# Constant matmuls ahead of the first transposes, and a new order of the first stage's roots, copies and modulation columns

## The reference

```python
c_act = jax.nn.silu(c)                                   # (1, 1024)
mod = c_act @ ada_w[layer] + ada_b[layer]                # (1, 6144)
sh1, sc1, g1, sh2, sc2, g2 = split(mod, 6)
h = rms_norm(x) * (1.0 + sc1) + sh1                      # x: (1024, 1024)
proj = h @ w_in                                          # queries, keys, values, output gate, 8 gate columns
```

## Time and profile before

| | us |
|---|---|
| three runs | 1089.71, 1090.55, 1092.70 (median 1090.55) |
| the profiled execution, its own time | 1091.59 |
| its span | 1089.7 |
| PE busy | 1074.5 (99%) |
| DVE busy | 727.2 (67%) |
| ACT busy | 447.5 (41%) |
| POOL busy | 168.1 (15%) |

### The profile page before, as it was taken

The page is one execution under the profiler, slowest core; times in us unless marked ns, Lnnn a source line. Parts: engine busy times, 40 slices in busy tenths (PEclk is TensorE's granted clock), DMA queues, the critical chain, the costliest instruction groups (busy, mean ns, idle before and its releaser), DMA issues.

```text
span 1089.7 us, 14684 instructions
## 1 busy us (share of the span) xinstructions
PE 1074.5 (99%) x5146; PEld 902.6 (83%) x5146; DVE 727.2 (67%) x1282; ACT 447.5 (41%) x824; POOL 168.1 (15%) x149
## 2 busy tenths in 40 slices
PE   6999999999999999999999999999999999999997
PEld 6888888888888888888888888888888888888886
DVE  6846767577479637888667665766666465844666
ACT  7852232222224316764343343334333325544445
POOL 3752322212326523310000000000000000000000
PEclk9999999999999999999999999999999999999999
DMA  9425352432432523115545435453553879665553
GB/s 377 170 77 162 116 197 80 140 114 61 160 116 64 189 78 129 66 39 203 158 142 198 169 107 192 146 168 131 191 177 106 299 270 395 223 194 193 192 155 155
DMA packets 86969, 177.10 MB, mean 163 GB/s; under 512 B 8152, under 2 KB 31320, under 8 KB 85872
## 3 DMA queue, kind: packets, MB, share of 16 engines
q1 hardware_dynamic: 85984, 174.80, 47.2%
q0 software_dynamic: 480, 1.09, 0.4%
q10 hardware_dynamic: 432, 0.27, 0.1%
HBM read 135.97 MB, written 40.16 MB: 162 GB/s over the span
## 4 chain that ended last, share of the span: by engine, by line
PE 97%; DVE 1%; ACT 1%; DMA 0%; issue 0%; DVEq 0%
PE OP L2360 27%; PE OP L2061 21%; PE O L2360 15%; PE ST L2360 5%; PE DC L2360 5%; PE AD L2360 5%; PE O L2061 3%; PE ST L2061 3%; PE AD L2061 2%; PE DC L2061 2%; PE O L2216 1%; PE O L2232 1%; PE DC L2232 1%; PE ST L2199 1%; PE OP L2135 1%; PE ST L2085 0%
## 5 line engine op out<-in xcount | busy, mean ns | idle before, releaser
L1826 DVE TENSOR_TENSOR dL<-dF,dH 128x1024 fp32r<-128x1024 f32 x77 | 93.0, 1223 | 69.1 <-ACT dH L1216 68.2
L2061 PE MATMUL OP<-wH,hH 128*128 128x512 f32 (+1 forms) x360 | 135.0, 375 | 0.1
L2061 PE MATMUL OP<-wH,hL 128*128 128x512 f32 (+1 forms) x360 | 132.1, 367 | 0.0
L2061 PE MATMUL OP<-wL,hH 128*128 128x512 f32 (+1 forms) x360 | 131.7, 366 | 0.0
L1216 ACT CAST dH<-dF 128x1024 fp32r<-128x1024 f32 x77 | 80.0, 1052 | 89.2 <-DMA dF<-w_units 42.6
L2360 PE MATMUL OP<-tH,wsH 128*128 128x512 f32 x264 | 102.7, 389 | 0.0
L2360 PE MATMUL OP<-tL,wsH 128*128 128x512 f32 x264 | 102.7, 389 | 0.0
L2360 PE MATMUL OP<-tH,wsL 128*128 128x512 f32 x264 | 102.7, 389 | 0.0
L2061 PEld LDWEIGHTS OP<-wH,hL 128*128 128x128 f32 x360 | 67.8, 188 | 11.3
L2061 PEld LDWEIGHTS OP<-wH,hH 128*128 128x128 f32 x360 | 67.9, 188 | 10.3 <-issue 0.3
L2061 PEld LDWEIGHTS OP<-wL,hH 128*128 128x128 f32 x360 | 67.9, 189 | 10.0
(11 more groups left out here) (341 smaller groups left out, 2645.5 us busy)
## 6 DMA issues: line engine op xcount, KB each, us to landing
raw<-w_units SPq DMA_DIRECT2D x76, 512.0 KB, 4.7
dF<-act_mid SPq DMA_DIRECT2D x77, 256.0 KB, 2.8
ada<-ada_rest SPq DMA_DIRECT2D x64, 256.0 KB, 2.9
wst<-w_units SPq DMA_DIRECT2D x44, 256.0 KB, 4.9
down_mid<-wst SPq DMA_DIRECT2D x22, 512.0 KB, 3.2
dF<-down_mid SPq DMA_DIRECT2D x44, 256.0 KB, 3.0
dF<-w_units SPq DMA_DIRECT2D x33, 256.0 KB, 6.1
ada<-ada_first SPq DMA_DIRECT2D x8, 1024.0 KB, 10.1
```

What stands on the lines that cost most here:

```text
L1826: nc.vector.tensor_tensor(dL[g][:], dF[g][:], dH[g][:].bitcast(F32), ALU.subtract).then_inc(d_L, 1)
L2061: ins = nc.tensor.matmul(out_ap, lhs[a], rhs[b], start=(n == 0 and i == 0), stop=(last and i == 2))
```

## The change

Five edits, all in the first stage:

- PE multiplies a tile of ones by itself 14 times (128 x 128 float32, into bank `OP0`, which the gates' products overwrite later), as soon as the constants stand and before it waits for row tile 0 (`WARM`).
- ACT does `root(t)` directly behind `square(t)`, ahead of the copy of row tile `t - 2`.
- The copy of row tile 7 out of the first bank goes from ACT to DVE, which then does both copies of that tile. DVE waits for ACT's copy of row tile 6 before it, since both count on one semaphore.
- The last product step and the closing addition of `sum1(1)` go behind DVE's three copies of row tiles 6 and 7.
- PE does `mod_columns(1)` behind the products of `k` = 0 and half 0, not ahead of them.

```diff
+WARM = 14
@@ ACT
                 square(t, xin[:, t, :])
+                root(t)
                 if t >= 2:
                     evac_xT(t - 2)
-                root(t)
             act.wait_ge(b1_ok, 1)
             mod_columns(0)
             modulate(0, 0)
             evac_xT(NT - 2)
-            evac_xT(NT - 1)
             modulate(0, 1)
@@ DVE
-            def evac_xT(t):
+            def evac_xT(t, j=1):
 
-                dve.wait_ge(n_tr, 2 * t + 2)
-                nc.vector.tensor_copy(four_of(xnT, 1, t),
-                                      XT_BANKS[2 * (t % 2) + 1][:].rearrange("p (k n) -> p k n",
-                                                                             n=P)).then_inc(xT_ok[1], 1)
+                dve.wait_ge(n_tr, 2 * t + j + 1)
+                nc.vector.tensor_copy(four_of(xnT, j, t),
+                                      XT_BANKS[2 * (t % 2) + j][:].rearrange("p (k n) -> p k n",
+                                                                             n=P)).then_inc(xT_ok[j], 1)
@@ DVE
-            sum1(1, 6)
+            sum1(1, 6, 7)
             evac_xT(NT - 2)
+            dve.wait_ge(xT_ok[0], NT - 1)
+            evac_xT(NT - 1, 0)
             evac_xT(NT - 1)
+            sum1(1, 7)
@@ PE
+                for _ in range(WARM):
+                    nc.tensor.matmul(OP[0][:, 0:P], ones[:], ones[:], start=True, stop=True)
                 for t in range(NT):
                     pe.wait_ge(n_hn, t + 1)
@@ PE
-                mod_columns(1)
                 pe.wait_ge(wg_L, 1)
@@ PE
                         if last:
                             ins.then_inc(gates_mm, 1)
+                        if k == 0 and half == 0:
+                            mod_columns(1)
```

## The result

| | before | changed |
|---|---|---|
| runs, us | 1089.71 to 1092.70, median 1091.09 (6) | 1092.86 to 1095.72, median 1094.99 (6) |
| profiled execution, own time | 1091.59 | 1092.86 |
| its span | 1089.70 | 1090.99 |

The ratio is 1.0034, 95% interval 1.0024 to 1.0044: slower by 3.7 us (2.6 to 4.8). I had forecast 1090.6 and a range of 1088.9 to 1092.2. The profiled execution of the changed kernel is the fastest of its six, 1.27 us over that of before. So its trace can show only a part of the loss; the mean granted clocks of the six are 0.999 for this one and 0.996 to 0.998 for the others.

What follows compares the result with a forecast made beforehand. TensorE was taken to bound the kernel (97% of the span). Terms -1.23, +1.16 and +0.12 gave +0.05 us on a median of 1090.55, so 1090.6, range 1088.9 to 1092.2.

Steps and rivals of the forecast that it cites:

- the paragraph on half 0: First products of k = 0: GpSimd's first weights land at 20.44 as before, products start at 25.65 against 26.88, 1.23 us earlier.
- the sum I had made: First stage: -1.23 (half 0 earlier), +1.16 (new wait ahead of k = 1), +0.12 (GpSimd's hL of k = 2), giving +0.05 us.
- The chain behind it: From first product at 25.65: moved columns at 27.60, ScalarE reads at 28.24, GpSimd starts at 30.24, k = 1 at 31.59.
- The fallen clock: TensorE idle between rows, products and k = 1: the clock falls between 24 and 32, costing 2.6 us, 1093.2; chance 0.09.
- the 5.3 us of the start: Slow-clock stretch after TensorE's first pass, to about 14.0; half speed that long was taken to cost 2.6 us.
- Constants done before row 0, rows 0 and 1 fast: TensorE's start: 28 constant passes end by 8.2, the clock rises at about 7.5, rows 0 and 1 save 2.5 us.
- Row 7's end at 23.8 to 24.3: TensorE's last row transposes end then, against 26.06 before.
- VectorE's copy of row 7 done by 24.6 to 24.9: Moved copy: bank full at 23.1 to 23.6, copies of rows 6 and 7 take 0.6 to 0.7 each.
- the constants don't do what they say: Rival: clock still rises at about 14, rows end as now, k = 1 at 32.0; 0.4 slower, 1091.0; chance 0.05.
- GpSimd as the bound for k = 2 and 3: Rival: GpSimd limits these products, everything some tenths later, +0.4 to +1.0, 1091.0 to 1091.5; chance 0.07.
- my 0.12: Term for GpSimd's hL of k = 2, adding 0.12 us to the forecast sum.

Runs made afterwards that it cites:

- the filled gap: The changed kernel plus 8 narrow constant matmuls on TensorE ahead of the first product: 1093.12, ratio 1.0019 against before.
- combination: Kernel before plus 4 wide constant matmuls, first weights loaded ahead of the second modulation tile, and 5 narrow constants behind row tile 7: 1092.61, ratio 1.0012.
- columns back: The changed kernel with mod_columns(1) ahead of the products again, the other four edits kept: 1092.56, ratio 1.0010 against before.

## Why the prediction was wrong

**The step that failed** is in the paragraph on half 0: "The weights land at 20.44 as before (the transfers ahead of them are issued in the same order, and none waits for anything that has moved)". The order was the same, but TensorE's own instructions come through the same DMA engines. The 56 instructions of the constants move its next 16 KB from 23.0 to 18.4, and the weights to 21.90. I had costed the 28 passes as time on an idle engine and never as code. Where the load is made harmless, by fewer instructions (25.87 and 31.64), the sum I had made comes true within 0.25 us for both starts (its rows end later than forecast, but off the path). It does not come true for the time: that kernel's median is still 1.1 us over before's, where I had summed 0.05. So the weights are the step that failed in the first stage, and not the whole of the miss.

**The chain behind it held.** From the start of the first product to k = 1 the forecast had 31.59 - 25.65 = 5.94 us, the changed kernel 33.06 - 27.29 = 5.77. The columns moved behind the products make every microsecond of lateness of the first product one of k = 1; with the constants alone the same late weights cost nothing (31.15). By the medians the constants alone cost nothing clear of the noise (ratio 1.0005) and the moved columns alone 1.0 us, against 3.7 for the whole change. No run has just these two edits together.

**The fallen clock** was my last rival, at 1093.2 and a chance of 0.09. It is probably the usual case of the changed kernel: ten of eleven executions have a mean clock of 0.998 or lower, nine of them are at 1093.9 or above, and the profile of one shows the fall. The mean alone doesn't settle it, since the clock is at half at the end of every execution as well: before, whose trace has no fall in the first stage, also reads 0.998. The size was overrated: 3.4 us at half speed, 1.7 us, of which 0.81 reached k = 1, where I had taken the 5.3 us of the start (2.6). Its chance was underrated: the late weights made the gap 2.2 to 3.1 us, where I had 1.85, but in other kernels here gaps of 1.83 and 1.64 were enough. The Trainium skill, TensorE: Matmul & The Clock Gate, section "A second HAM failure mode: psum-queue depth-cycling", warned of short idle times between groups of matmuls. The traces agree in that the clock read 0.50 after single gaps of 3.08, 1.99, 1.83 and 1.64 us. But it did not fall after the 2.16 us of the execution of 1092.86, so the length of the gap alone doesn't decide.

**The rest.** Constants done before row 0, rows 0 and 1 fast: right. Row 7's end at 23.8 to 24.3: 23.07 + 1.8 = 24.9 where its tile was late, 23.74 in the execution where it wasn't. VectorE's copy of row 7 done by 24.6 to 24.9: near 26.0 in the first of these, 24.1 in the second. Without the constants it begins only at 26.0, so for slow rows I had set the steps ahead of it too low. The 0.3 to 0.4 for "the constants don't do what they say" was 1.1 without them. GpSimd as the bound for k = 2 and 3: k = 1 to the columns of k = 4 is 41.12 - 33.06 = 8.06 after, 39.55 - 31.66 = 7.89 before, so 0.17 us more, near my 0.12.

In sum: of 3.7 us, 1.4 are k = 1 starting late (weights, passed on by the moved columns), which the execution of 1092.86 shows alone. About 1.7 go with the clock: the filled gap takes them away, and within one kernel the executions of lower mean clock are 1.8 (constants only), 1.8 (combination) and 1.1 us (columns back) longer by the medians of the groups. The trace of a fall accounts for only 0.8 of it at k = 1; the rest of what that trace lost to the faster one lies near 535 and 935, and its cause is open. The last 0.6 or so I can't place.

**Open:** why several medians are 0.7 to 1.1 us worse than the traces explain (the columns moved alone, the one-column constants, the wide constants in the changed kernel); what lengthens the wait near 935; and whether it is row tile 7, late or on time, that makes an execution keep its clock. The roots and the moved copy were not tried each by itself.

## What to carry to other kernels

Instructions added to an idle engine are not free where transfers are tight: they move that engine's code loads, and it is worth looking in the trace for which transfer the next one will land on. If an idle time of TensorE is to be filled, few wide matmuls bring less code than many narrow ones. To fill up to the very start of the real work keeps the clock up, but it paid only in one of the two tries (1.7 us in the changed kernel, nothing in the kernel before with wide constants). Put a short piece that a chain over other engines waits for ahead of long independent work: with the two narrow matmuls behind eight wide ones, k = 1 started 5.77 us after the first product both at 27.29 and at 25.87. And a profile shows one execution: here two of one kernel differed by 1.8 us, and most of that stood outside the stage that was changed. The version that beats both kernels here is the kernel before with three wide constant matmuls: 1090.36, and 1090.34 with a filled gap, against 1091.36 (ratios 0.9989 and 0.9987, both clear of 1, but small).

## What the hardware showed that was not expected

- One 16 KB packet of instructions among full data queues delayed a transfer of 512 KB by 1.0 to 1.5 us (20.44 to 21.44, 21.86 and 21.90). Of two executions of one kernel, one had two such transfers late and the other only the second (row tile 7 taken at 20.58 and 19.04).
- The clock fell back to 0.50, from 9.0 to 12.4, after the wide constants had ended at 6.7, 2 us before row 0.
- Of 1.7 us of work lost to the fallen clock, an idle time behind it took in half: k = 1 was 0.81 us later.
- More work on TensorE made the changed kernel 1.7 us faster (the filled gap).
